# A two-layer decoder step on one core: GpSimd's and VectorE's orders in the FFN's first steps, the sums of squares at sub-layer ends, and the recurrence's projection quarters two by two

## The chip, the cores and the metric

The kernel runs on one core of a Trainium2 chip. The metric is the time of one execution on the device in microseconds. Each engine (TensorE or PE, VectorE or DVE, ScalarE or ACT, GpSimd or POOL, SyncE or SP) runs its own program in the order in which it is written; engines meet at semaphores only.

## The reference, cut

Two layers, 544 tokens (512 of a prompt and 8 x 4 of a sample group), D = 1024, FFN width 2816, all float32. Layer 0 mixes by causal pooling, layer 1 by a gated delta rule.

```python
for i in range(DEPTH):                                   # DEPTH = 2
    ng = p['norm_gains'][i]
    x = x + 0.5 * rmsnorm(swiglu(rmsnorm(x, ng[0]), gate[i, 0], up[i, 0], down[i, 0]), ng[1])
    h = rmsnorm(x, ng[2])
    y = pool_mixer(h, ...) if i % 2 == 0 else gated_deltanet(h, ...)
    x = x + rmsnorm(y, ng[3])
    x = x + 0.5 * rmsnorm(swiglu(rmsnorm(x, ng[4]), gate[i, 1], up[i, 1], down[i, 1]), ng[5])

def swiglu(h, w_gate, w_up, w_down):
    return (jax.nn.silu(h @ w_gate) * (h @ w_up)) @ w_down
```

The gated delta rule projects h to q, k, v, z (each head 128 wide), runs a short convolution, then for each chunk of tokens solves a triangular system and carries a state of 128 x 128 per head:

```python
v_new = ui - wi @ state
o = (qi * exp(gi)) @ state + ai @ v_new
state = state * exp(g_last) + k_dec.T @ v_new
```

## The kernel before

**Products.** Every float32 product w h is made of three reduced-precision matmuls: w_high h_high, w_low h_high, w_high h_low. A high part is a rounded copy that ScalarE writes (round_op L1635 for weights into w_h, high_quarter L1698 for activations into hhi); a low part is the difference of the value and its high part, one subtraction on GpSimd (low_of, L886) or VectorE (low_of, L2164; low_quarter, L2298, into hlo). Which of the two makes a weight's low part is said by by_vector. Tokens are worked in two halves of 272 (hf 0 and 1).

**Sub-layers.** There are six, r = 0 to 5: FFN (r = 0), pooling mixer (1), FFN (2), FFN (3), delta rule (4), FFN (5). The four FFNs are e = 0 to 3. An FFN is a list of steps. Step 0 is the first gate product (first_gate, L1074), steps 1 to 3 are plain products up, gate, up (plain, L1107), steps 4 to 7 the first chunk of the down projection (down, L1146). All later gate and up products go by a Strassen scheme with seven products in place of eight (seven, L1128). This needs three differences of quarters of the normed input, t1 to t3: VectorE makes tf (difference, L2292), ScalarE rounds it (high_difference, L1689), GpSimd makes its low part t_l (low_difference, L891). While the plain steps run, VectorE also applies the norm (normed, L2287), multiplies gate and up results (plain_gate L2269, plain_up L2273 and L2276, into hidf), makes the low part of the hidden values (hidden_low, L2282) and evicts down products (L2243 and L2245).

**Sub-layer ends.** For the RMSNorm after a sub-layer, ScalarE squares each of the 16 result tiles (L1654), VectorE adds most of the squares (add_square, L2206 and L2209, counted by ADDS), and TensorE sums over partitions by f32 matmuls with a matrix of 1/D: add_early (L1041) takes VectorE's sum, add_late (L1046) single squares. ScalarE makes the inverse root of it (post_root, L1599 and L1601), VectorE applies it and adds to x (post, L2228 and L2232). In the last down steps of every FFN the two halves are worked one after the other (down_halves, L1164), with the sums of half 0 among the products of half 1; `late_downs` lets VectorE evict the last four tiles between the pairs of post's operations. low_part (L2188) then makes the next sub-layer's hlo, low_first the low parts of the next FFN's step 0.

**The delta rule.** The projections are cut into quarters of 12 matmuls (quarter, L1344). A list `plan` gives for each quarter the steps of the recurrence that belong to its position, 48 positions for a group of four heads: level_z and level_ux (L1424, L1433, L1437) solve the triangular system by levels, right_side and keys_by_token (L1454, L1456) and new_values (L1463) carry the state, o_norm is L1483, low_products and att_products L1413, l2_sum L1397, and steps whose name begins with s_ belong to the sample group (s_update L1563). ScalarE, VectorE and GpSimd walk the same plan in an order of their own.

Of the kernel before, what the change touches and what calls it, by code (L numbers as in the profile page):

```python
# [129 lines left out]
def by_vector(step, i):  # L130
    return i in (A11, A22) if step.seven else step is steps_of(step.e)[0]


def low_counts():
    ops, ends, differences, pool, dve = [], [], [], 0, 0
    for step in STEPS:
# [8 lines left out]
        if at in (2, 3):  # L145
            for _ in range(4 - at):
                pool += 1
                differences.append(pool)
# [19 lines left out]
def build(nc, consts, I, O):  # L168
# [5 lines left out]
    with ctx:  # L174
# [337 lines left out]
        ADDS = [0, None, 10, 20, 30, 40]  # L512
# [356 lines left out]
        def _(pool):  # L869
# [23 lines left out]
            def ffn(e, r):  # L893
                steps = steps_of(e)
                for step in steps:
# [137 lines left out]
        def _(pe):  # L1033
# [5 lines left out]
            def add_early(r, hf):  # L1039
                pe.wait_ge(ss_add, ADDS[r] + ((9, 10) if r in (1, 4) else (8, 10))[hf])  # L1040
# [25 lines left out]
            def first_gate(step, r, late, freed):  # L1066
# [14 lines left out]
                for hf in range(2):  # L1081
# [71 lines left out]
            def down_halves(steps, r):  # L1153
                for hf in range(2):
                    for mt in range(4, KT):
# [3 lines left out]
                        for k in range(step.tiles):  # L1159
# [138 lines left out]
            def delta():  # L1298
# [64 lines left out]
                for at in range(len(plan)):  # L1363
                    quarter(at)
# [229 lines left out]
        def _(act):  # L1594
# [61 lines left out]
            def ffn(e, r):  # L1656
# [34 lines left out]
                def high_quarter(n):  # L1691
# [5 lines left out]
                    src = tf[:, 0] if n == 1 else y[:, ks, cols(hf)]  # L1697
# [462 lines left out]
        def _(dve):  # L2160
# [5 lines left out]
            def low_first(e, m):  # L2166
                for i in (2 * m, 2 * m + 1):
# [33 lines left out]
            def add_square(r, n):  # L2201
                mt, hf = TILES_F[n]
                before = ADDS[r] + (n - 3 if n < 9 else 7 if n == 9 else (8 if n == 12 else 9))
# [43 lines left out]
            def late_downs(e, r):  # L2247
                def between(k):
# [3 lines left out]
                    if k >= 4:  # L2252
                        add_square(r, n - 2)
                    if k == 4 and e == 1:
                        low_first(2, 0)
                return between

            def ffn(e, r):
# [26 lines left out]
                def normed(hf):  # L2285
                    for k in range(KT):
# [3 lines left out]
                def difference(n, a, b):  # L2290
                    dve.wait_ge(x_add, X_ADDS[r] + 18 + n)
                    dve.tensor_tensor(tf[:, n % 2 if n < 3 else 0], a, b, ALU.subtract).then_inc(x_add, 1)  # L2292

                def low_quarter(n):
                    ks, hf = ((slice(0, HK4), 0), (slice(0, HK4), 1), (slice(HK4, KT), 1), (slice(HK4, KT), 0))[n]
                    src = tf[:, 0] if n == 1 else y[:, ks, cols(hf)]
# [7 lines left out]
                for hf in range(2):  # L2304
# [7 lines left out]
                for n in range(1, 4):  # L2312
                    plain_up(steps[1], n // 2, n % 2)
                for n in range(4):
                    hidden_low(steps[1], n, n)
# [6 lines left out]
                for n in range(4):  # L2322
                    hidden_low(steps[3], n, n)
                dve.wait_ge(lo_pool, LOW_DIFFERENCES[3 * e + 2])
# [455 lines left out]
            for m in range(2):  # L2780
                low_first(0, m)
# [4 lines left out]
            for m in range(2):  # L2786
                low_first(1, m)
# [5 lines left out]
            post(2, 0, late_downs(1, 2))  # L2793
            low_part(3, 0)
            low_first(2, 1)
# [5 lines left out]
            low_first(3, 0)  # L2801
# [61 lines left out]
```

## Time and profile before

| what | value |
| --- | --- |
| median of 3 runs | 2488.42 us (2485.8 to 2612.95) |
| the profiled execution | 2487.07 us |
| its span in the trace | 2485.3 us |
| busy: PE, DVE, ACT, POOL | 94%, 65%, 43%, 45% of the span |
| TensorE's granted clock, mean | 0.975 of full speed |
| HBM | 207.20 MB read, 27.93 MB written |

The span is the trace's time from first to last instruction; 1.8 us of the execution lie outside it. The granted clock is the share of TensorE's full speed (2.4 GHz) that the chip allowed; its lower level is 1.2 GHz, 0.5 in such a column. A wait is the idle time of an engine, put down to the instruction that ended it.

### The profile page before, as it was taken

The numbers are of one execution on the slowest core, as the hardware profiler recorded it, in microseconds if no ns is written. First come the engines' busy times: TensorE is split into PE (matmuls) and PEld (weight loads), VectorE is DVE, ScalarE is ACT, GpSimd is POOL, SyncE is SP. The second block draws the span as 40 slices with busy tenths as digits, with TensorE's granted clock in tenths as the row PEclk, the third lists the DMA queues.
The fourth block names the chain that finished last, engine by engine and source line by source line (L and its number), as shares of the span: only waits on it lengthen the run. The fifth ranks groups of instructions, "written<-read, shape, count | busy, mean of one in ns | idle before, by whom it ended". The sixth has DMA issues, their size and how long they took to land. (4 is left out here: it accounts for less than half of the span.)

```text
span 2485.3 us, 45038 instructions
## 1 busy us (share of the span) xinstructions
PE 2332.6 (94%) x17619; PEld 2237.7 (90%) x17619; DVE 1627.3 (65%) x3004; ACT 1070.9 (43%) x2192; POOL 1107.6 (45%) x841
## 2 busy tenths in 40 slices
PE   7899999689999998999997899999999998899998
PEld 6899998589999988999986898888987987899997
DVE  5685584768585676765845666758567438686585
ACT  4353343334343453443446455363452224353343
POOL 2565562046565626655632022241223642665562
PEclk9999999899999999999999999999999999999999
DMA  3233323013333312332322434425445341233322
GB/s 121 63 104 98 102 82 104 20 43 100 114 104 109 96 59 79 106 97 86 99 75 63 112 84 120 126 59 133 127 118 146 101 158 61 73 94 98 103 81 75
DMA packets 294604, 235.57 MB, mean 95 GB/s; under 512 B 37339, under 2 KB 284788, under 8 KB 294107
## 3 DMA queue, kind: packets, MB, share of 16 engines
q1 hardware_dynamic: 294395, 232.71, 30.8%
q8 instruction: 141, 2.31, 0.4%
q14 instruction: 68, 0.56, 0.1%
HBM read 207.20 MB, written 27.93 MB: 95 GB/s over the span
## 5 line engine op out<-in xcount | busy, mean ns | idle before, releaser
L886 POOL TENSOR_TENSOR w_l<-raw,w_h 128x512 fp32r<-128x512 f32 (+1 forms) x416 | 522.1, 1275 | 330.9 <-ACT w_h L1635 330.9
L886 POOL TENSOR_TENSOR w_l<-wsum,w_h 128x512 fp32r<-128x512 f32 x216 | 332.6, 1548 | 364.3 <-ACT w_h L1635 364.3
L1146 PE MATMUL acc<-hid,w_h 128*128 128x272 f32 x2432 | 461.2, 288 | 8.4 <-DVE y L2243 8.4
L1635 ACT ACTIVATE w_h<-raw 128x512 fp32r<-128x512 f32 (+1 forms) x576 | 323.3, 585 | 166.2 <-PE acc L1146 113.7
L1146 PEld LDWEIGHTS acc<-hid,w_h 128*128 128x128 f32 x2432 | 382.8, 188 | 10.7 <-issue 10.7
L1146 PE MATMUL acc<-hid,w_l 128*128 128x272 f32 x1216 | 349.4, 287 | 0.0
L2245 DVE TENSOR_TENSOR y<-acc,y 128x272 f32<-128x272 f32 x192 | 84.7, 441 | 253.6 <-PE acc L1146 230.9
L1635 ACT ACTIVATE w_h<-wsum 128x512 fp32r<-128x512 f32 x216 | 134.9, 625 | 259.6 <-DVE wsum L2180 243.9
L1146 PEld LDWEIGHTS acc<-hid,w_l 128*128 128x128 f32 x1216 | 228.9, 188 | 0.0
L1344 PE MATMUL acc<-hhi,dhi 128*128 128x272 f32 (+1 forms) x1040 | 197.4, 311 | 13.0 <-POOL hlo L1022 3.7
L1685 ACT ACTIVATE hid<-hidf 128x272 fp32r<-128x272 f32 x176 | 75.2, 427 | 293.4 <-DVE hidf L2368 192.5
L2164 DVE TENSOR_TENSOR w_l<-raw,w_h 128x512 fp32r<-128x512 f32 x160 | 178.7, 1128 | 34.8 <-ACT w_h L1635 32.9
L1128 PE MATMUL acc<-hlo,w_h 128*128 128x272 f32 x624 | 180.2, 289 | 0.0
L1128 PE MATMUL acc<-hhi,w_l 128*128 128x272 f32 x624 | 179.7, 288 | 0.0
L1128 PE MATMUL acc<-hhi,w_h 128*128 128x272 f32 x624 | 179.5, 288 | 0.0
L1344 PE MATMUL acc<-hlo,dhi 128*128 128x272 f32 (+1 forms) x1040 | 178.1, 293 | 0.5 <-POOL hlo L924 0.4
L1344 PEld LDWEIGHTS acc<-hhi,dhi 128*128 128x128 f32 (+1 forms) x1040 | 149.3, 194 | 31.4 <-issue 14.4
L1344 PE MATMUL acc<-hhi,dlo 128*128 128x272 f32 (+1 forms) x1040 | 177.6, 294 | 0.0
L1128 PE MATMUL aux<-t_l,w_h 128*128 128x272 f32 x528 | 152.9, 290 | 0.0
L1128 PE MATMUL aux<-hlo,w_h 128*128 128x272 f32 x528 | 152.9, 290 | 0.0
L1128 PE MATMUL aux<-t_h,w_h 128*128 128x272 f32 x528 | 152.7, 289 | 0.0
L1344 PEld LDWEIGHTS acc<-hlo,dhi 128*128 128x128 f32 (+1 forms) x1040 | 150.5, 192 | 2.1 <-POOL hlo L924 1.5
(334 smaller groups left out, 6153.0 us busy)
## 6 DMA issues: line engine op xcount, KB each, us to landing
raw<-in_w_ffn_gate_dram SPq DMA_DIRECT2D x44, 1024.0 KB, 5.1
raw<-in_w_ffn_up_dram SPq DMA_DIRECT2D x44, 1024.0 KB, 5.1
raw<-in_w_ffn_down_dram SPq DMA_DIRECT2D x48, 768.0 KB, 4.4
wraw<-in_dn_w_in_dram SPq DMA_DIRECT2D x48, 512.0 KB, 4.0
raw<-in_w_ffn_down_dram SPq DMA_DIRECT2D x16, 512.0 KB, 3.3
room<-in_state_delta_dram SPq DMA_DIRECT2D x16, 512.0 KB, 4.8
out_delta_sample_dram<-room SPq DMA_DIRECT2D x16, 512.0 KB, 4.2
wraw<-in_dn_w_out_dram SPq DMA_DIRECT2D x16, 512.0 KB, 5.1
```

The costliest lines, as they stand in the source:

```text
L886: pool.tensor_tensor(w_l[o % RING][:, 0:n, :], source(step, i), w_h[o % RING][:, 0:n, :].bitcast(F), ALU.subtract)\
L1128: last = pe.matmul(banks[b], w[o % RING][:, k, :], h[:, k, :], start=(k == 0 and n == 0), stop=(k == HK4 - 1 and n == 2))
L1146: last = pe.matmul(acc[m][:, hf, 0:HT], w[o % RING][:, k % HK4, :], hid[:, k, z, cols(hf)], start=(k == 0 and j == 0), stop=(k == step.til ...
L1344: mm = pe.matmul(into[0:width, hf, 0:HT], w[s][:, kw, 0:width], a[:, ka, cols(hf)], start=(k == first and i == 0), stop=(k == last and i = ...
L1635: act.activation(w_h[o % RING][:, 0:n, :], source(step, i), ACT.Copy).then_inc(op_hi, 1)
L1685: act.activation(hid[:, tile, 0, cols(hf)], hidf[:, s, :], ACT.Copy).then_inc(hid_hi, 1)
L2164: dve.tensor_tensor(w_l[o % RING][:, 0:n, :], source(step, i), w_h[o % RING][:, 0:n, :].bitcast(F), ALU.subtract).then_inc(lo_dve, 1)
L2245: dve.tensor_tensor(yt, src, yt, ALU.add).then_inc(comb, 1)
```

## The change

- by_vector: of step 0's four weight low parts VectorE makes two and GpSimd two (before, VectorE all four). low_first has two operations, and its place moves: it no longer stands inside post.
- low_difference on GpSimd: t_l of differences 0 and 1 behind step 3's low parts (before, step 2's), of difference 2 behind step 4's (before, step 3's).
- The squares: VectorE adds those of tiles 2 to 9 only; TensorE takes tiles 12 to 15 by add_late, and add_early of half 1 and add_late 11 move into down_halves, each one place earlier.
- first_gate: the second tile's w_h product stands ahead of the first tile's w_l product.
- VectorE in the plain steps: plain_up of step 1 in the middle of the norm of half 1, each hidden_low right behind its hidden; difference 2 moves from ahead of step 3's ups to behind its last hidden_low. ScalarE: high_difference 2 and high_quarter 0 move behind step 3's hidden values and ahead of step 5's weights.
- TensorE in the delta rule: at even positions two quarters, at odd ones none; the steps keep their positions.

```diff
 def by_vector(step, i):
-    return i in (A11, A22) if step.seven else step is steps_of(step.e)[0]
+    return i in (A11, A22) if step.seven else step is steps_of(step.e)[0] and i < 2
...
-        ADDS = [0, None, 10, 20, 30, 40]
+        ADDS = [0, None, 8, 16, 24, 34]
...
-                    if step is steps[2]:
+                    if step is steps[3]:
                         low_difference(r, 0)
                         low_difference(r, 1)
-                    if step is steps[3]:
+                    if step is steps[4]:
                         low_difference(r, 2)
...
-                    pe.wait_ge(*low_ready(a + 1))
-                    products(0, hf, w_l, hhi)
                     pe.wait_ge(op_hi, b + 2)
                     freed(1, hf)
                     products(1, hf, w_h, hhi)
+                    pe.wait_ge(*low_ready(a + 1))
+                    products(0, hf, w_l, hhi)
                     products(0, hf, w_h, hlo, h_lo)
...
                             if hf and mt == 4 and k == HK4 - 1:
                                 add_late(r, 10)
+                                add_late(r, 11)
                             if hf and mt == 5 and k == 1:
-                                add_late(r, 11)
+                                add_early(r, 1)
...
             def sums_end(r):
-                add_early(r, 1)
-                add_late(r, 14)
-                add_late(r, 15)
+                for n in range(12, 16):
+                    add_late(r, n)
...
                 for at in range(len(plan)):
-                    quarter(at)
+                    if at % 2 == 0:
+                        quarter(at)
+                        quarter(at + 1)
                     for step, g, c in plan[at]:
...
-                high_difference(2)
                 for n in range(4):
                     hidden(steps[3], n, 2 * n + 2)
+                high_difference(2)
+                high_quarter(0)
                 for i in range(2):
                     round_op(steps[5], i)
-                high_quarter(0)
...
-                    if k >= 4:
-                        add_square(r, n - 2)
-                    if k == 4 and e == 1:
-                        low_first(2, 0)
...
-                    normed(hf)
+                    normed(hf, range(0, HK4))
+                    if hf:
+                        plain_up(steps[1], 0, 0)
+                    normed(hf, range(HK4, KT))
+                plain_up(steps[1], 0, 1)
                 difference(0, b12, b11)
-                plain_up(steps[1], 0, 0)
+                hidden_low(steps[1], 0, 0)
+                plain_up(steps[1], 1, 0)
                 difference(1, b22, tf[:, 0])
...
+                for n in range(4):
+                    plain_up(steps[3], n // 2, n % 2)
+                    if n:
+                        hidden_low(steps[3], n - 1, n - 1)
+                hidden_low(steps[3], 3, 3)
                 dve.wait_ge(lo_pool, LOW_DIFFERENCES[3 * e])
                 difference(2, b22, b12)
-                for n in range(4):
-                    plain_up(steps[3], n // 2, n % 2)
-                for n in range(4):
-                    hidden_low(steps[3], n, n)
-                dve.wait_ge(lo_pool, LOW_DIFFERENCES[3 * e + 2])
+                dve.wait_ge(lo_pool, LOW_DIFFERENCES[3 * e + 1])
                 difference(3, b21, tf[:, 1])
...
-            low_first(3, 0)
-            post(4, 0, lambda k: low_first(3, 1) if k == 4 else None)
+            low_first(3)
+            post(4, 0)
```

GpSimd's program at the first FFN, before: low parts of weights (w_l) and of the differences (t_l).

```order
L886 TENSOR_TENSOR w_l<-raw,w_h 128x512 x8
L891 TENSOR_TENSOR t_l<-tf,t_h 128x1088 x2
L886 TENSOR_TENSOR w_l<-raw,w_h 128x512 x4
L891 TENSOR_TENSOR t_l<-tf,t_h 128x1088
L886 TENSOR_TENSOR w_l<-raw,w_h 128x512 x8
```

The same rows in the changed kernel:

```order
L886 TENSOR_TENSOR w_l<-raw,w_h 128x512 x14
L891 TENSOR_TENSOR t_l<-tf,t_h 128x1088 x2
L886 TENSOR_TENSOR w_l<-raw,w_h 128x512 x2
L891 TENSOR_TENSOR t_l<-tf,t_h 128x1088
L886 TENSOR_TENSOR w_l<-raw,w_h 128x512 x6
```

The two t_l in a row stand six low parts later (two of these are step 0's, the others step 3's), and the third stands two low parts behind them, in place of four.

VectorE's program at the end of the first FFN's plain steps, before: the last product of step 3, its low parts, difference 3, low_quarter (hlo) and the evictions of step 4 (COPY).

```order
L2273 TENSOR_TENSOR hidf<-acc,stat 128x272
L2276 TENSOR_TENSOR hidf<-hidf,g 128x272
L2282 TENSOR_TENSOR hid<-hidf,hid 128x272 x4
L2292 TENSOR_TENSOR tf<-y,tf 128x1088
L2298 TENSOR_TENSOR hlo<-y,hhi 128x4x272
L2243 COPY y<-acc 128x272 x2
L2298 TENSOR_TENSOR hlo<-tf,hhi 128x4x272
```

The same place in the changed kernel, whose lines have other numbers (L2280 is hidden_low, L2290 difference, L2296 low_quarter, L2245 the copy):

```order
L2271 TENSOR_TENSOR hidf<-acc,stat 128x272
L2274 TENSOR_TENSOR hidf<-hidf,g 128x272
L2280 TENSOR_TENSOR hid<-hidf,hid 128x272 x2
L2290 TENSOR_TENSOR tf<-y 128x1088
L2290 TENSOR_TENSOR tf<-y,tf 128x1088
L2296 TENSOR_TENSOR hlo<-y,hhi 128x4x272
L2245 COPY y<-acc 128x272 x2
L2296 TENSOR_TENSOR hlo<-tf,hhi 128x4x272
```

Difference 2 now stands here, directly ahead of difference 3; two of the four hidden_low have left the stretch for an earlier place.

TensorE's program in a group of the recurrence, before, from level_ux of one position to the quarter two positions later (acc0 from dhi and dlo is a quarter, L1391 the tails, L1463 new_values, L1405 decay_sum).

```order
L1433 MATMUL aux1<-room 128x128 x4
L1437 MATMUL aux0<-room 128x128 x4
L1391 MATMUL acc1<-cst,y 27x128 x2
L1344 MATMUL acc0<-hhi,dhi1 128x272 x4
L1344 MATMUL acc0<-hhi,dlo1 128x272 x4
L1344 MATMUL acc0<-hlo,dhi1 128x272 x4
L1463 MATMUL aux1<-room 128x128 x4
L1405 MATMUL acc1<-cst,gates 128x128 x4
L1344 MATMUL acc0<-hhi,dhi0 128x272 x4
L1344 MATMUL acc0<-hhi,dlo0 128x272 x4
L1344 MATMUL acc0<-hlo,dhi0 128x272 x4
```

The same steps in the changed kernel, where level_ux is L1435 and L1439, the tails L1393, new_values L1465, decay_sum L1407:

```order
L1435 MATMUL aux1<-room 128x128 x4
L1439 MATMUL aux0<-room 128x128 x4
L1393 MATMUL acc1<-cst,y 27x128 x2
L1465 MATMUL aux1<-room 128x128 x4
L1407 MATMUL acc1<-cst,gates 128x128 x4
L1344 MATMUL acc0<-hhi,dhi0 128x272 x4
L1344 MATMUL acc0<-hhi,dlo0 128x272 x4
L1344 MATMUL acc0<-hlo,dhi0 128x272 x4
L1344 MATMUL acc0<-hhi,dhi0 128x272 x4
L1344 MATMUL acc0<-hhi,dlo0 128x272 x4
L1344 MATMUL acc0<-hlo,dhi0 128x272 x4
```

The quarter between level_ux and new_values is gone; it stands with its neighbour, ahead of this stretch, and the next two quarters follow one another behind decay_sum.

## Rows read from the trace of the kernel before

**Rows 1.** The page, part 1: busy us, share of the span, instructions.

```profile
PE 2332.6 (94%) x17619; PEld 2237.7 (90%) x17619; DVE 1627.3 (65%) x3004; ACT 1070.9 (43%) x2192; POOL 1107.6 (45%) x841
```

**Rows 2.** TensorE's waits over the span: total us, times, longest us.

```profile
PE acc L1107 <- POOL w_l L886: 16.9, 4, 4.3
PE acc L1074 <- ACT hhi L1613: 16.8, 13, 4.1
PE aux L1041 <- DVE stat L2209: 9.9, 3, 3.3
PE aux L1563 <- DVE room L2713: 8.5, 3, 3.5
PE acc L1146 <- DVE y L2243: 8.4, 8, 1.7
PE acc L1397 <- ACT stat L1976: 5.9, 4, 2.5
PE acc L1107 <- DVE hidf L2273: 5.6, 4, 1.5
PE acc L1074 <- DVE w_l L2164: 3.1, 1, 3.1
```

**Rows 3.** Windows, FFN 2's steps 2, 3: us, busy by engine, PEclk, DMA, GB/s.

```profile
921.00:937.50 16.50, 12.29 (x96) 12.07 (x96) 8.40 (x17) 9.36 (x17) 8.56 (x5) 0.93 0.03 10
937.60:951.95 14.35, 14.35 (x98) 14.35 (x99) 2.77 (x7) 1.29 (x3) 7.50 (x5) 0.84 0.23 74
```

**Rows 4.** Timeline of GpSimd there: start us, us, line, operation, count, idle before.

```profile
928.94 5.01 POOL L891 TENSOR_TENSOR t_l<-tf,t_h 128x1088 fp32r<-128x1088 f32 x2 [10.47 <-ACT t_h L1689]
933.90 6.02 POOL L886 TENSOR_TENSOR w_l<-raw,w_h 128x512 fp32r<-128x512 f32 x4
939.89 2.50 POOL L891 TENSOR_TENSOR t_l<-tf,t_h 128x1088 fp32r<-128x1088 f32 x1
```

**Rows 5.** Timeline of VectorE, same stretch and columns.

```profile
933.69 1.41 DVE L2292 TENSOR_TENSOR tf<-y 128x1088 f32<-128x1088 f32 x1
...
952.83 1.49 DVE L2282 TENSOR_TENSOR hid<-hidf,hid 128x272 fp32r<-128x272 f32 x4
954.24 2.39 DVE L2292 TENSOR_TENSOR tf<-y,tf 128x1088 f32<-128x1088 f32 x1
956.56 2.39 DVE L2298 TENSOR_TENSOR hlo<-y,hhi 128x1088 fp32r<-128x1088 f32 x1
```

**Rows 6.** Timeline of ScalarE, same stretch.

```profile
954.33 1.10 ACT L1698 ACTIVATE hhi<-y 128x1088 fp32r<-128x1088 f32 x1
```

**Rows 7.** Timeline of TensorE at the end of sub-layer 3.

```profile
1271.96 0.62 PE L1046 MATMUL aux<-stat,cst 128*128 128x272 f32 x2
...
1281.87 0.73 PE L1041 MATMUL aux<-stat,cst 128*128 128x272 f32 x2 [3.30 <-DVE stat L2209]
```

**Rows 8.** Timeline of VectorE at the ends of sub-layers 2 and 3.

```profile
882.79 1.28 DVE L2164 TENSOR_TENSOR w_l<-raw,w_h 128x512 fp32r<-128x512 f32 x2
...
1273.58 0.92 DVE L2228 SCALAR_TENSOR_TENSOR aux<-y,gpost,aux 128x272 f32<-128x272 f32 x2 [4.89 <-ACT aux L1601]
...
1275.45 0.90 DVE L2228 SCALAR_TENSOR_TENSOR aux<-y,gpost,aux 128x272 f32<-128x272 f32 x2
...
1279.17 0.43 DVE L2209 TENSOR_TENSOR stat<-stat 128x272 f32<-128x272 f32 x1
```

**Rows 9.** Timeline of TensorE in the recurrence, group 1.

```profile
1446.52 0.75 PE L1344 MATMUL acc<-hhi,dhi 128*128 128x272 f32 x4
...
1448.11 1.05 PE L1463 MATMUL aux<-room 128*128 128x128 f32 x8
...
1521.15 1.16 PE L1413 MATMUL acc<-x 128*128 128x128 f32 x8 [0.27 <-DVE room L2614]
```

**Rows 10.** Timeline of VectorE in the recurrence, group 1.

```profile
1447.19 0.68 DVE L2650 TENSOR_TENSOR room<-room,aux 128x512 f32<-128x512 f32 x1
...
1520.42 0.69 DVE L2614 TENSOR_TENSOR room<-acc,room 128x512 f32<-128x512 f32 x1
```

More of the change, by code:

```diff
@@ L144, in low_counts @@
         ends.append((pool, dve))
-        if at in (2, 3):
-            for _ in range(4 - at):
+        if at in (3, 4):
+            for _ in range(5 - at):
                 pool += 1
@@ L1039, in add_early @@
             def add_early(r, hf):
-                pe.wait_ge(ss_add, ADDS[r] + ((9, 10) if r in (1, 4) else (8, 10))[hf])
+                pe.wait_ge(ss_add, ADDS[r] + ((9, 10) if r in (1, 4) else (8, 6))[hf])
                 pe.matmul(aux[hf][:, 0:HT], ones_mean, ssacc[:, hf, :], start=True, stop=False)
@@ L1696, in high_quarter @@
                         act.wait_ge(x_add, X_ADDS[r] + 22)
-                    src = tf[:, 0] if n == 1 else y[:, ks, cols(hf)]
+                    src = tf[:, 1] if n == 1 else y[:, ks, cols(hf)]
                     act.activation(hhi[:, ks, cols(hf)], src, ACT.Copy).then_inc(h_hi, 1)
@@ L2164, in low_of, with low_first @@
                 dve.tensor_tensor(w_l[o % RING][:, 0:n, :], source(step, i), w_h[o % RING][:, 0:n, :].bitcast(F), ALU.subtract).then_inc(lo_dve, 1)
-            def low_first(e, m):
-                for i in (2 * m, 2 * m + 1):
+            def low_first(e):
+                for i in range(2):
                     low_of(steps_of(e)[0], i)
@@ L2202, in add_square @@
                 mt, hf = TILES_F[n]
-                before = ADDS[r] + (n - 3 if n < 9 else 7 if n == 9 else (8 if n == 12 else 9))
+                before = ADDS[r] + (n - 3 if n < 9 else 7)
                 dve.wait_ge(y_sq, 16 * r + n + 1)
@@ L2283, in hidden_low, with normed @@
                        .then_inc(hid_lo, 1)
-                def normed(hf):
-                    for k in range(KT):
+                def normed(hf, ks):
+                    for k in ks:
                         dve.scalar_tensor_tensor(y[:, k, cols(hf)], x[:, k, cols(hf)], gain(r // 3, 2 * (r % 3), k), rpre[:, hf, :],
@@ L2307, in ffn @@
                         plain_gate(steps[0], m, hf)
-                    normed(hf)
+                    normed(hf, range(0, HK4))
[3 more added lines that the diff above has]
+                plain_up(steps[1], 0, 1)
                 difference(0, b12, b11)
-                plain_up(steps[1], 0, 0)
+                hidden_low(steps[1], 0, 0)
+                plain_up(steps[1], 1, 0)
                 difference(1, b22, tf[:, 0])
-                for n in range(1, 4):
-                    plain_up(steps[1], n // 2, n % 2)
-                for n in range(4):
-                    hidden_low(steps[1], n, n)
+                hidden_low(steps[1], 1, 1)
+                plain_up(steps[1], 1, 1)
+                hidden_low(steps[1], 2, 2)
+                hidden_low(steps[1], 3, 3)
                 for n in range(4):
                     plain_gate(steps[2], n // 2, n % 2)
+                for n in range(4):
[3 more added lines that the diff above has]
+                hidden_low(steps[3], 3, 3)
                 dve.wait_ge(lo_pool, LOW_DIFFERENCES[3 * e])
                 difference(2, b22, b12)
-                for n in range(4):
-                    plain_up(steps[3], n // 2, n % 2)
-                for n in range(4):
-                    hidden_low(steps[3], n, n)
-                dve.wait_ge(lo_pool, LOW_DIFFERENCES[3 * e + 2])
+                dve.wait_ge(lo_pool, LOW_DIFFERENCES[3 * e + 1])
                 difference(3, b21, tf[:, 1])
@@ L2779, in _ @@
             low_part(0, 0)
-            for m in range(2):
-                low_first(0, m)
+            low_first(0)
             low_part(0, 1)
@@ L2785, in _ @@
             pool_mixer()
-            for m in range(2):
-                low_first(1, m)
+            low_first(1)
             for hf in range(2):
@@ L2793, in _ @@
             post(2, 0, late_downs(1, 2))
+            low_first(2)
             low_part(3, 0)
-            low_first(2, 1)
             post(2, 1)
```

4 lines of the change are left out of this document (2 added, 2 removed).

## The prediction

> **What bounds the kernel now.** I read the page's engine table first. TensorE is busy 94% of the span and VectorE 65% [rows 1], so time can only come from TensorE's gaps, and everything that makes TensorE wait anew costs its full length. The list of TensorE's waits [rows 2] names the gaps by line. Those that the change touches are: L1107 on GpSimd's low parts, 16.9 us in 4 waits, one in each FFN; L1107 on VectorE's hidf, 5.6 us in 4; L1146 on VectorE's y, 8.4 us in 8, two in each FFN; L1041 on the sum of squares, 9.9 us in 3; and part of L1074's 16.8 us on hhi. In the recurrence the list has short waits behind ScalarE (ACT) and VectorE (DVE) (L1397, L1563), each a few microseconds in all. That is the point to keep: the recurrence's steps are covered nearly everywhere today, and the cover is what the last part of the change rearranges.
>
> A wait can cost more than its length. In the windows of FFN 2, step 2 has 96 matmuls in 12.29 us busy, and step 3, which begins after the 4.2 us wait on GpSimd, has 98 records in 14.35 us at a mean granted clock of 0.84 [rows 3]: the clock stood at its lower level of 1.2 GHz for a part of it. The price of the drop is 14.35 - 12.29 = 2.06 us, so that wait costs about 6.3 us in each FFN.
>
> **The plain part.** Why the wait is there: GpSimd takes two t_l differences (5.01 us for 2) at 928.94, and only then step 3's low parts [rows 4]. The change puts these two differences one step later and lets GpSimd do its low parts first, and VectorE's operations on hidf come earlier. Removed in each FFN: 5.6 / 4 = 1.4 us on hidf, 16.9 / 4 = 4.23 us on w_l, 2.06 us of clock; 7.7 us.
>
> What is late next is step 5. Let T be the end of step 3. Then VectorE still has the last hidden and its low part (one of the four in the 1.49 us), ending at about T + 1.3 to 1.9; difference(2) now starts there (1.41 us alone [rows 5]), T + 3.2; ACT rounds it (1.1 us, as the activation of the same size in [rows 6]), T + 4.35; GpSimd's L891 takes 2.5 us [rows 4], T + 6.9. Only then come step 5's two low parts, at most 6.02 / 4 = 1.5 us each [rows 4]; I take 2.5 for both, T + 9.4. TensorE has step 4 to do, half a plain step, 12.29 / 2 = 6.1 us. So TensorE waits about 3.4 us before step 5, where it waited 8.4 / 4 = 2.1 us for y in two pieces, of which the longest is 1.7; the second one, 0.4, I take at 0.9. Given back: 3.4 - 1.7 + 0.9 - 0.4 = 2.2 us. A wait of 3.4 us is near the 4.2 us one in length, so I charge it the same 2.06 us of clock. Net 7.7 - 2.2 - 2.0 = 3.5 us in each FFN, **14 us** in four. Bounds: 22 us if the clock holds, nothing if VectorE's operations at that point stay as slow as today. They are slow: difference(3) takes 2.39 us where difference(2) takes 1.41 at the same size [rows 5], while GpSimd works.
>
> That row is where the Trainium skill bears: "SBUF — State Buffer", section "Who interferes with whom", says that a VectorE instruction with two SBUF inputs contends with a GpSimd instruction that reads SBUF. The trace agrees, with 2.39 against 1.41 us. By that rule the two low_quarter operations and GpSimd's L891 would again stand one behind the other in the new order, and the gain would be at the lower end of my bounds.
>
> **The boundaries.** At the end of an FFN VectorE runs a chain: post-norm, evictions of the last tiles, adds of squares, 1.86 us for each pair of tiles; TensorE's first use of the sum waits 3.30 us for it [rows 7]. Three edits shorten it. add_late 11 moves from 1271.96 [rows 7] up beside add_late 10, past 12 matmuls of the down projection, 12 x 12.29 / 96 = 1.5 us; ACT's root waits for it and VectorE's chain starts at 1273.58 behind that root [rows 8], so the chain starts up to 1.5 us earlier. Two add_squares of 0.35 us each (0.43 with their overlap [rows 8]) leave VectorE, one of them ahead of the last eviction. TensorE does two more f32 matmuls instead, 0.62 us each as the one at 1271.96 [rows 7] with its overlap, inside the gap. So 3.30 us shrinks by about 2.5: that is three places (the sub-layers 0, 3 and 5), 7.5 us. At sub-layer 2 the first two low parts, 1.28 us at 882.79 [rows 8], also leave the chain for after it: 3 us, less possible blocking of the hlo operations by GpSimd's two added low parts, so 3 with bounds 1.5 and 4. Before the last FFN two low parts leave the chain as well (1.2 us of the 16.8 in L1074's waits [rows 2]). At the start TensorE waits 3.1 us for VectorE's w_l [rows 2]; with two of the four on GpSimd and the second w_h product ahead I take 1.1. Sum 7.5 + 3 + 1.2 + 1.1 = 12.8, say **13 us**; bounds 7 and 18.
>
> **The recurrence.** Today each position is one quarter of a projection (12 matmuls) and then the steps of the recurrence for that position. At even positions the change sets two quarters, then the steps of both positions back to back. Merging saves nothing by itself: the matmuls are the same and run without gaps either way. What it changes is the distance between dependent steps. From an odd to the next even position the cover doubles; from an even to the odd one it goes: a quarter is 1.59 us (1446.52 to 1448.11 [rows 9]).
>
> Two pairs can be read. level_ux(2) to new_values(0): L1463 starts behind the quarter at 1448.11; without the quarter it could start at 1446.52, but VectorE's L2650, which makes its operand, starts at 1447.19 and takes 0.68 [rows 10], so it starts at about 1447.9: lost 1.3. att_products(0) to att_products(1): the second L1413 waits 0.27 us already with a quarter between [rows 9]; the bank is freed by L2614 at 1520.42 + 0.69 [rows 10]; lost about 1.6 to 1.7. Of the other even-to-odd pairs with a dependence I price right_side(1) to o_norm(0) and level_ux(7) to o_norm(2) at 0.65 each and s_products at 0.3, between 0 and the 1.59 of a quarter, near the 0.68 of a one-tile operation [rows 10] as each has one such operation between. Two more, level_ux(6) to new_values(2) and s_inverse to s_level_z, would lose 1.2 and 1.5, but a wait of 1.1 to 3.5 us on ACT or VectorE stands right behind (L1397, L1563 [rows 2]) and swallows it. So 1.3 + 0.65 + 0.65 + 0.3 + 1.7 = 4.6 us in each of three steady groups, 13.8. The first group, which waits for ACT anyway, loses nothing. In the last one the pairs of the sample's state (s_state to s_right_side, s_new_values to s_outputs) stand at odd distance one too, and no such wait covers them: about 8. Sum **21.5 us** lost; bounds 0 (all of it under waits that exist) and 40 (each charged a whole quarter, and the clock drops too).
>
> **Sum.** The profiled execution took 2487.07 us, 1.35 below the median of three. 2487.07 - 14 - 13 + 21.5 = 2481.6; I say **2481**. A measurement of this kernel can tell about 2% from no change, 49.8 us: below 2438.7 or above 2538.2.
>
> **Rivals.**
> - *The recurrence loses nothing.* The new short waits only eat the time that TensorE now waits behind ACT and VectorE, whose orders are unchanged. For it: waits of 5.9 and 8.5 us exist there [rows 2]. Against: TensorE is nearly gapless between them, and VectorE's answer comes 0.68 us and more after it starts. 2487.07 - 27 = 2460.
> - *Slower: the recurrence's new waits cost more than both other parts gain.* The place is the even-to-odd pairs; the point is 27 us. If each lost pair cost a whole quarter, and some of these gaps also brought the lower clock as the one of 4.2 us does [rows 3], it would lose 40 us: 2487.07 - 27 + 40 = 2500. The Trainium skill has a rule that speaks for this: "TensorE: Matmul & The Clock Gate", section "A second HAM failure mode: psum-queue depth-cycling", describes frequent small idles between matmul groups that let the clock swing between its two levels. The trace speaks against it so far: the recurrence has gaps of 0.3 us [rows 9] to 3.5 us [rows 2] already, and the drop that I priced stands behind one of 4.2 us.
> - *The plain part moves its wait and gains nothing.* The L891 of difference(2) and step 5's low parts take GpSimd 5 to 5.5 us after T + 4.35; with VectorE's blocked operations between, step 5 waits 7 us with the lower clock. Then 2487.07 - 13 + 21.5 = 2495.5, slower too.
> - *The change doesn't do what it says.* The orders show the quarters in pairs and GpSimd's differences moved, so this has no weight.
>
> **Chances.** The forecast's case, 2470 to 2490: 0.42. The recurrence loses nothing: 0.20. The recurrence loses 40: 0.16. The plain part gains nothing: 0.14. Something else, either side: 0.08. For 8 in 10 the range goes from 2457 (the first rival with 3 us more from the boundaries) to 2504 (the second with 4 us more lost); the likeliest case's own range is 2470 to 2490. All named cases lie within 2%; faster and slower by over 2% get 0.04 each from the rest.
>
> **What would show it.** Right: L1107 no longer waits for w_l or hidf; a wait of some 3.4 us stands before step 5 (L1146 in the new kernel too), on w_l rather than y; L1041's 3.3 us waits are gone, with L1046 waiting briefly for ACT's square; new waits of 1 to 2 us before new_values, att_products and o_norm, some 5 us in each steady group; clock 1.0 in step 3's window. Wrong: no new waits in the recurrence (first rival), a clock well below 0.98 there (second), or a wait at step 5 of 6 us and more (third).

## The result, and the profile after

The changed kernel takes 2497.31 us (median of 20 runs) against 2488.56 us before (20 runs). The ratio is 1.0034, 95% interval 1.0023 to 1.0044: slower by 0.3%, some 8 us, where I had forecast 6 us faster. The profiled execution took 2491.7 us, 4.6 above the one before. The changed kernel's single runs lie wider apart (2491.45 to 2506.98, one disturbed run left out) than those before (2485.43 to 2496.57, two left out), so a difference of 4 us between two medians says little below; the ratios carry the verdicts. The profiled run is one of the three shortest, so the trace shows about half of the 8 us.

That small number hides two large ones. The windows of the six stages of the changed kernel, cut at the first matmul of each (first FFN, pooling mixer, second and third FFN, delta rule, last FFN; the columns are start and end, length, then busy time of PE, PEld, DVE, ACT and POOL, the granted clock, DMA share and GB/s):

```profile
19.40:415.60 396.20, 387.88 (x3031) 383.91 (x3030) 269.79 (x482) 174.20 (x358) 217.12 (x161) 1.00 0.30 93
415.60:472.00 56.40, 37.32 (x136) 27.50 (x134) 40.52 (x74) 16.59 (x37) 5.72 (x5) 0.86 0.07 22
472.00:863.00 391.00, 385.17 (x2982) 381.23 (x2983) 274.57 (x495) 174.85 (x359) 217.31 (x161) 0.98 0.29 92
863.00:1259.80 396.80, 392.38 (x3048) 387.22 (x3046) 277.84 (x496) 176.71 (x360) 226.07 (x169) 0.99 0.28 86
1259.80:2082.00 822.20, 738.39 (x5377) 674.19 (x5376) 468.47 (x918) 340.89 (x710) 224.00 (x184) 0.95 0.37 106
2082.00:2489.20 407.20, 393.43 (x3030) 387.63 (x3030) 283.51 (x515) 177.36 (x363) 220.07 (x163) 0.98 0.27 86
```

The same six windows of the kernel before:

```profile
20.40:429.60 409.20, 392.75 (x3026) 387.81 (x3026) 271.95 (x486) 174.63 (x357) 218.69 (x161) 0.98 0.28 90
429.60:484.30 54.70, 36.84 (x136) 26.98 (x134) 39.74 (x76) 16.01 (x36) 1.95 (x3) 0.87 0.05 14
484.30:881.70 397.40, 387.11 (x2981) 382.55 (x2982) 272.58 (x489) 173.67 (x356) 218.76 (x161) 0.98 0.29 92
881.70:1289.30 407.60, 392.65 (x3041) 386.73 (x3039) 279.62 (x507) 178.05 (x363) 225.05 (x167) 0.99 0.27 84
1289.30:2069.60 780.30, 722.51 (x5378) 660.80 (x5376) 472.09 (x918) 344.39 (x710) 223.71 (x184) 0.97 0.39 111
2069.60:2485.30 415.70, 393.06 (x3026) 386.92 (x3026) 285.04 (x519) 177.60 (x363) 219.26 (x161) 0.98 0.27 85
```

The four FFNs with their ends gain 13.0, 6.4, 10.8 and 8.5 us, the start 1 and the mixer loses 1.7: 38 us gained. The delta rule goes from 780.3 to 822.2 us, 42 lost. Its two parts can be read from the same rows: the time in which TensorE is not busy goes from 780.30 - 722.51 = 57.8 to 822.20 - 738.39 = 83.8 us, 26 more; the same number of matmuls is busy for 15.9 us longer, and the mean clock falls from 0.97 to 0.95.

TensorE's waits in the changed kernel, to be held against [rows 2] (line numbers two or more higher: L1465 is new_values, L1485 o_norm, L1415 low_products and att_products, L1514 s_level_z, L1565 s_update, L1399 l2_sum):

```profile
PE acc L1146 <- POOL w_l L886: 13.7, 5, 3.3
PE acc L1074 <- ACT hhi L1615: 13.0, 12, 4.1
...
PE aux L1514 <- ACT spare L2055: 10.5, 4, 2.9
PE aux L1465 <- DVE room L2654: 9.8, 8, 1.5
...
PE acc L1415 <- DVE room L2618: 8.3, 4, 3.0
...
PE aux L1565 <- DVE room L2717: 6.3, 3, 2.6
PE acc L1344 <- DVE dlo L2520: 5.6, 5, 2.3
...
PE aux L1485 <- ACT room L2013: 4.5, 8, 0.6
```

L1107's waits on GpSimd and on hidf are gone, and so is L1041's on the squares. Step 5's wait for w_l (L1146) has come, 3.3 us in each FFN. New in the recurrence are the waits of L1465 and L1485. The quarters (L1344) waited for dlo, the low part of their weights, before as well, 2.8 us in 2 times; three times of 1.0 us have come to it. The waits of L1514 and L1415 are longer (4.5 and 4.0 us before), and L1565's is shorter (8.5 before).

### The profile page after: what moved, and what is told of

It is laid out like the page before. It is cut to its first block and busy times, and to the rows that moved or that the text cites. A ratio compares the mean times of both kernels' runs of the same rounds, so it can differ in the third digit from the quotient of the medians.

```text
span 2489.2 us, 45054 instructions
## 1 busy us (share of the span) xinstructions
PE 2342.0 (94%) x17635; PEld 2247.2 (90%) x17635; DVE 1621.0 (65%) x2988; ACT 1067.1 (43%) x2192; POOL 1113.0 (45%) x849
## 3 DMA queue, kind: packets, MB, share of 16 engines
q8 instruction: 141, 2.31, 0.4%
## 5 line engine op out<-in xcount | busy, mean ns | idle before, releaser
L1146 PE MATMUL acc<-hid,w_h 128*128 128x272 f32 x2432 | 465.9, 290 | 13.7 <-POOL w_l L886 13.7
L1146 PEld LDWEIGHTS acc<-hid,w_h 128*128 128x128 f32 x2432 | 387.6, 191 | 14.8 <-POOL w_l L886 14.8
L1146 PE MATMUL acc<-hid,w_l 128*128 128x272 f32 x1216 | 352.4, 290 | 0.0
L1146 PEld LDWEIGHTS acc<-hid,w_l 128*128 128x128 f32 x1216 | 232.0, 191 | 0.0
L1344 PE MATMUL acc<-hhi,dhi 128*128 128x272 f32 (+1 forms) x1040 | 198.5, 314 | 17.0 <-DVE dlo L2520 5.6
L2166 DVE TENSOR_TENSOR w_l<-raw,w_h 128x512 fp32r<-128x512 f32 x152 | 173.4, 1149 | 34.8 <-ACT w_h L1637 32.9
L1344 PEld LDWEIGHTS acc<-hhi,dhi 128*128 128x128 f32 (+1 forms) x1040 | 156.3, 201 | 35.6 <-issue 16.2
L1344 PE MATMUL acc<-hhi,dlo 128*128 128x272 f32 (+1 forms) x1040 | 182.2, 299 | 0.0
L1344 PE MATMUL acc<-hlo,dhi 128*128 128x272 f32 (+1 forms) x1040 | 181.5, 298 | 0.5 <-POOL hlo L924 0.4
L1344 PEld LDWEIGHTS acc<-hhi,dlo 128*128 128x128 f32 (+1 forms) x1040 | 155.9, 199 | 0.5
L1344 PEld LDWEIGHTS acc<-hlo,dhi 128*128 128x128 f32 (+1 forms) x1040 | 154.3, 197 | 1.9 <-POOL hlo L924 1.4
```

Of the source, the lines that this page charges most:

```text
L1146: last = pe.matmul(acc[m][:, hf, 0:HT], w[o % RING][:, k % HK4, :], hid[:, k, z, cols(hf)], start=(k == 0 and j == 0), stop=(k == step.til ...
L1344: mm = pe.matmul(into[0:width, hf, 0:HT], w[s][:, kw, 0:width], a[:, ka, cols(hf)], start=(k == first and i == 0), stop=(k == last and i = ...
L2166: dve.tensor_tensor(w_l[o % RING][:, 0:n, :], source(step, i), w_h[o % RING][:, 0:n, :].bitcast(F), ALU.subtract).then_inc(lo_dve, 1)
```

## The experiments

**e1 and e2: the pairs alone, and all but the pairs.** e1 is the changed kernel with

```diff
-                    if at % 2 == 0:
-                        quarter(at)
-                        quarter(at + 1)
+                    quarter(at)
```

> The changed kernel with the quarters one by one again (everything else of the change kept). Theory: the pairs alone make the recurrence longer, by waits of the dependent steps (about 26 us) and by TensorE's lower clock behind them (about 16 us); then the recurrence is 780 us again, L1465 on DVE and L1485 on ACT have no waits, and the time is 2487.1 - 38 = 2449 us. Rival: the recurrence is slower for another reason (what the FFN leaves behind, the chip's state): it stays near 822 us and the time near 2491.

Measured: 2455.38 us, ratio 0.9865 (0.9848 to 0.9882). The delta rule takes 783.7 us, 38 less than in the changed kernel and 3 more than before; new_values and o_norm (L1463 and L1483 here) are not in the list of waits.

e2 is the kernel before with those three lines the other way round.

> The kernel before with the pairs of quarters alone. Theory: +42 us in the recurrence and nothing elsewhere, 2487.1 + 42 = 2529 us. Rival (the pairs cost only the waits that I priced in the prediction): + 21.5, 2509 us. Rival (the two parts work on each other): the recurrence differs from the 822 us that it took in the changed kernel by over 5 us.

Measured: 2535.64 us, ratio 1.0195 (1.0174 to 1.0215), some 48 us; the profiled execution, the shortest of the four runs, 2529.27, 42 above the one before, and its delta rule takes 822.1 us against 822.2 in the changed kernel. The pairs make the whole loss, and the delta rule's loss doesn't depend on what the rest of the change does. My price for it, 21.5 us, is out.

Windows of the delta rule, cut at s_decay of each of the four groups, show where it lies. The first is the start, the next three are the steady groups, the last is the end. First before:

```profile
1289.30:1499.42 210.12, 186.11 (x1337) 171.92 (x1335) 122.62 (x233) 110.30 (x238) 38.87 (x35) 0.94 0.33 91
1499.42:1657.58 158.16, 149.60 (x1131) 136.16 (x1130) 106.69 (x196) 75.64 (x158) 40.71 (x36) 0.98 0.41 111
1657.58:1814.52 156.94, 148.30 (x1132) 135.68 (x1131) 105.73 (x196) 75.52 (x158) 40.90 (x36) 0.99 0.41 112
1814.52:1967.03 152.51, 143.75 (x1095) 131.96 (x1094) 94.29 (x189) 51.94 (x95) 55.37 (x44) 0.98 0.46 132
1967.03:2069.60 102.57, 94.75 (x688) 85.09 (x687) 42.75 (x104) 31.00 (x61) 47.87 (x36) 0.98 0.38 122
```

and with the whole change:

```profile
1259.80:1473.41 213.61, 186.54 (x1336) 172.44 (x1335) 122.95 (x233) 109.64 (x238) 38.85 (x34) 0.93 0.32 90
1473.41:1640.73 167.32, 153.26 (x1132) 139.35 (x1131) 106.65 (x196) 74.62 (x159) 40.67 (x36) 0.96 0.39 105
1640.73:1808.01 167.28, 153.22 (x1132) 139.33 (x1131) 106.70 (x196) 74.62 (x159) 40.68 (x36) 0.96 0.39 105
1808.01:1972.23 164.22, 147.12 (x1095) 134.91 (x1095) 89.61 (x189) 51.27 (x96) 55.91 (x45) 0.95 0.42 123
1972.23:2082.00 109.77, 98.24 (x688) 88.17 (x687) 42.57 (x104) 30.74 (x61) 47.89 (x36) 0.95 0.35 114
```

The start loses 3.5 us, the three groups 9.2, 10.3 and 11.7, the end 7.2. In the first steady group TensorE stands still for 8.6 us before and for 14.1 us after, 5.5 more; I had priced 4.6. But the same matmuls are busy 3.7 us longer as well, at a lower clock, and for that I had charged nothing. In the changed kernel TensorE's timeline has it within this group:

```profile
1421.23 1.13 PE L1465 MATMUL aux<-room 128*128 128x128 f32 x8 [1.25 <-DVE room L2654]
...
1506.05 0.41 PE L1514 MATMUL aux<-spare 32*32 32x32 f32 x8 [2.95 <-ACT spare L2055]
...
1507.80 1.11 PE L1344 MATMUL acc<-hhi,dlo 128*128 128x272 f32 x4
...
1510.47 0.67 PE L1344 MATMUL acc<-hhi,dlo 128*128 128x272 f32 x4
...
1537.36 1.02 PE L1344 MATMUL acc<-hhi,dhi 128*128 128x272 f32 x4 [1.02 <-DVE dlo L2520]
1538.18 1.11 PE L1344 MATMUL acc<-hhi,dlo 128*128 128x272 f32 x4
```

The wait before new_values (L1465) is 1.25 us, where I had 1.3. The one before L1514, which I had let L1563's wait swallow, is 2.95 us, 1.5 more than before, and behind it a row of four matmuls takes 1.11 us instead of 0.67 until 1510.5: the granted clock is 0.50 from 1507 to 1510, TensorE's lower level of 1.2 GHz. The quarter at 1537.36 shows a wait that I had not thought of at all: its weights are not split yet. VectorE's timeline, before (L2701 and L2516) and after (L2705 and L2520, the split into dlo):

```profile
1547.97 0.29 DVE L2701 TENSOR_TENSOR spare<-spare,aux 128x128 f32<-128x128 f32 x1
...
1555.19 1.21 DVE L2516 TENSOR_TENSOR dlo<-wraw,dhi 128x1024 fp32r<-128x1024 f32 x1
```
```profile
1528.87 0.29 DVE L2705 TENSOR_TENSOR spare<-spare,aux 128x128 f32<-128x128 f32 x1 [2.12 <-PE aux L1528]
...
1536.10 1.21 DVE L2520 TENSOR_TENSOR dlo<-wraw,dhi 128x1024 fp32r<-128x1024 f32 x1
```

The quarter is the first of its pair and stands behind the same matmuls as before. What has moved is the step of an even position, s_state (L1528): it now stands behind both quarters of its pair. VectorE waits 2.12 us for it where it did not wait before, and the split, which ends 8.4 us behind that answer in both kernels, ends at 1537.31. Between s_state and this quarter TensorE has four quarters now and had five. So this is lost cover too, by way of VectorE's order. The clock falls behind that wait as well.

**e3: pairs only where nothing depends.**

```diff
-                    if at % 2 == 0:
+                    if (at // 2 * 2 - 4) % 48 in (10, 14, 20, 24, 26, 28, 30, 36, 38):
+                        quarter(at)
+                    elif at % 2 == 0:
```

> The changed kernel with pairs only where the odd position's steps need nothing from the even one's (single quarters at positions 10, 14, 20, 24, 26, 28, 30, 36 and 38 of each group). Theory (a pair costs only by the cover it takes from a dependent step): like the kernel without pairs, 2449 us, within 4. Rival (a pair costs or saves by itself, by longer bursts, evictions or the clock): off from that kernel by over 6 us.

Measured: 2459.46 us, ratio 0.9880 (0.9865 to 0.9896) against 0.9865 for e1: at the edge of the interval, 4 us in the medians and 4.3 in the delta rule (788.0 against 783.7). The theory holds to that size: the nine pairs that take the cover of a dependent step carry 34 of the 38 us by which the delta rules of the changed kernel and of e1 differ (822.2 against 783.7). My list of them had a hole, though: the trace of e3 has a wait of 1.5 us at level_ux (L1437 there) on VectorE in each of the three steady groups, which neither e1 nor the changed kernel has. No gain shows from the pairs that are left.

**e7: single quarters at positions 28 and 30 only.** The same edit as e3 with the list (28, 30).

> The changed kernel with single quarters at positions 28 and 30 of each group only. Theory (the longer wait before L1514, 2.9 us, brings the lower clock behind it, the one of 1.4 us before did not): in each steady group the wait of att_products goes from 1.8 to 0.3 and that of L1514 from 2.9 to 1.4, and the 3.3 us at 1.2 GHz behind it go too, 4.7 us in each of three groups, 14 in all: 2497 - 14 = 2483 us. Rival (the clock falls for another reason, such as the longer bursts): the low stretch stays, and 9 us are gained, 2488.

Measured: 2487.79 us, ratio 0.9998 (0.9986 to 1.0009) against 1.0034, some 9 us less; in the trace the delta rule takes 815.0 us, 7.2 less. The group's window is

```profile
1476.06:1639.67 163.61, 151.87 (x1131) 137.82 (x1131) 107.77 (x196) 74.62 (x159) 39.52 (x36) 0.97 0.40 107
```

3.7 us shorter than in the changed kernel: 2.3 us less idle (11.74 against 14.06) and 1.4 us less busy. I had expected 4.7. L1514's wait (L1516 here) is back at 1.47 us, and the low clock behind it is gone, here and in the second steady group; the wait for att_products only went from 1.8 to 1.0. In the third steady group the clock still falls, 7 us behind the same wait (1.45 us there), after matmuls at full speed:

```profile
1833.03 0.41 PE L1516 MATMUL aux<-spare 32*32 32x32 f32 x8 [1.45 <-ACT spare L2057]
...
1841.02 1.11 PE L1344 MATMUL acc<-hlo,dhi 128*128 128x272 f32 x4
```

So the time is the one that the rival gave, 2488; its sign, a low stretch that stays, is there in one group of three. That the longer wait brings the low clock is shown for two groups, and the 14 us that I had built on it were too many.

**e8: pairs at odd positions.**

```diff
-                    if at % 2 == 0:
+                    if at == 0:
+                        quarter(at)
+                    elif at % 2:
```

> The changed kernel with pairs at odd positions: two quarters, then the steps of an odd and the next even position. Theory (a pair costs by the steps whose cover it takes): now even-to-odd neighbours have two quarters between them and odd-to-even ones none; new_values, o_norm and the first pair of att_products no longer wait, but s_level_z to s_level_u and the second pair of att_products do, about 3 to 4 us in each group: between, 2465 to 2475 us. Rival (pairs cost by the bursts or by earlier claims on weights and banks, whatever the parity): 2490 or more.

Measured: 2479.54 us, ratio 0.9964 (0.9949 to 0.9979), profiled 2471.98; the delta rule takes 801.8 us. Half of the loss goes with the parity. What stays is not what I had named: neither s_level_u nor the second att_products leads its list, but quarters, which wait 2.35 us for dlo in two groups, 3.4 and 3.7 us for ScalarE at the end of a group, and in all 3.5 us longer than before for hlo. Here the first quarter of a set of weights does stand one position earlier than before. These quarters' waits are 14 us longer than before, while TensorE's idle time is 11.6 us longer in all, since others shrank, and its matmuls are busy 9.8 us longer. So most of the waiting that stays is theirs and not lost cover of steps; but new_values and o_norm, which I had freed of waits, still wait 2.9 and 2.2 us in all (9.8 and 4.5 in the changed kernel).

**e4 and e5: the plain part alone, the boundaries alone.** e4 has the change's edits to low_difference, difference, plain_up, hidden_low and ScalarE's order; e5 those to by_vector, ADDS, add_early, add_late, first_gate and low_first.

> The kernel before with the change's plain part alone (GpSimd's differences one step later, VectorE's and ScalarE's orders). By the prediction's price, 3.5 us in each FFN, 14 in all: 2473 us. By the stages of the changed trace, where the FFNs and their ends gained 38 us together and the ends were priced at 13: 25 us, 2462. Step 5 waits 3.3 us for w_l in either case; they differ in whether the lower clock follows.

Measured: 2470.91 us, ratio 0.9931 (0.9911 to 0.9950), 17 us: nearer to the prediction's price than to the stages'.

> The kernel before with the change's boundary edits alone (step 0's low parts, the squares, first_gate, low_first). By the prediction's price 13 us: 2474. By difference (the kernel without pairs against the plain part alone) 11 to 16 us, so 2471 to 2476. Rival (the two parts overlap: what one gains the other would have gained too): less than 8.

Measured: 2473.01 us, ratio 0.9941 (0.9922 to 0.9959), 15 us. The two add up to the 33 us of e1. One part of e5 goes the wrong way: the mixer's stage takes 56.4 us here and 54.4 in e4. VectorE's and GpSimd's timelines in e5 say why:

```profile
446.50 2.58 DVE L2739 TENSOR_TENSOR winv<-hp 128x1356 f32<-128x1356 f32 x1
```
```profile
446.39 3.81 POOL L886 TENSOR_TENSOR w_l<-raw,w_h 128x512 fp32r<-128x512 f32 x2
```

The two low parts that by_vector gave to GpSimd fall into the mixer, and the operation beside them takes 2.58 us, where later ones of the same line take 1.55 to 1.57.

**e6: the third difference still later.** e1 with

```diff
-        if at in (3, 4):
-            for _ in range(5 - at):
+        if at in (3, 5):
+            for _ in range(2 if at == 3 else 1):
...
-                    if step is steps[4]:
+                    if step is steps[5]:
                         low_difference(r, 2)
```

> The changed kernel with single quarters, and GpSimd's third difference behind step 5's low parts in place of step 4's. Theory (step 5 waits 3.3 us only because L891 stands ahead of its low parts on GpSimd): that wait goes in all four FFNs, 13 us, and with it the lower clock behind three of them, some 5 us: 2455.4 - 18 = 2437 us. Rival (VectorE's low_quarter, or the evictions behind it, are late as well): TensorE waits for y or hlo in its place, and at most 5 us are gained, 2450.

Measured: 2450.19 us, ratio 0.9842 (0.9821 to 0.9863), which overlaps e1's. The rival's time was right, its cause was not: TensorE still waits for w_l in the first place (9.0 us in 8 times, 2.1 us for y). Step 5's wait falls from 3.3 to 1.83 us, as ScalarE rounds step 5's weights only behind its two other operations, and up to 1 us comes back at the tiles behind.

**e9 and e10: weights rounded earlier, the mixer's low parts back, the difference last.** e9 is e6 with

```diff
-    return i in (A11, A22) if step.seven else step is steps_of(step.e)[0] and i < 2
+    return i in (A11, A22) if step.seven else step is steps_of(step.e)[0] and (i < 2 or step.e == 1)
...
-                for n in range(4):
+                for n in range(3):
                     hidden(steps[3], n, 2 * n + 2)
-                high_difference(2)
-                high_quarter(0)
                 for i in range(2):
                     round_op(steps[5], i)
+                hidden(steps[3], 3, 8)
+                high_difference(2)
+                high_quarter(0)
...
-                for i in range(2):
+                for i in range(4 if e == 1 else 2):
                     low_of(steps_of(e)[0], i)
```

> The kernel of e6 (single quarters, third difference behind step 5's low parts) with two more edits: ScalarE rounds step 5's weights ahead of the last hidden of step 3, so that GpSimd makes their low parts while step 4 runs; and at the FFN behind the pooling mixer VectorE makes all four of step 0's low parts again, so that GpSimd works on none of them beside the mixer's VectorE operations. Theory: step 5 no longer waits for w_l (1.8 us in each FFN) but for y, 1.3 to 1.7 us, as it did before the change; the pooling mixer's stage goes from 56.4 us back to 54.7, as L2739 takes 1.56 us again and not 2.58: 2450.2 - 1.7 - 1 to 4 = 2444 to 2448 us. Rival for the mixer (its longer stage comes from the earlier start, not from GpSimd's port): it stays at 56.4 and TensorE waits 3.3 us at L1279 as before.

Measured: 2452.17 us, ratio 0.9862 (0.9841 to 0.9882): no better than e1. The mixer's half of it worked: 54.4 us, and L2746 (L2739 above) takes 1.56 us. The other half turned against itself. GpSimd's, VectorE's and TensorE's timelines in the first FFN of e9:

```profile
84.31 2.54 POOL L891 TENSOR_TENSOR t_l<-tf,t_h 128x1088 fp32r<-128x1088 f32 x1 [3.67 <-ACT t_h L1689]
```
```profile
85.27 2.73 DVE L2295 TENSOR_TENSOR hlo<-y,hhi 128x1088 fp32r<-128x1088 f32 x1 [0.79 <-ACT hhi L1698]
88.04 0.79 DVE L2244 COPY y<-acc 128x272 f32<-128x272 f32 x2
```
```profile
88.63 0.36 PE L1146 MATMUL acc<-hid,w_h 128*128 128x272 f32 x1 [3.40 <-DVE y L2244]
```

With the low parts out of the way GpSimd starts L891 early enough to meet low_quarter (L2295), as it did in the changed kernel and did not in e6, where low_quarter takes 1.29 us. That ends behind L891, at 88.0, and the evictions that TensorE waits for stand behind it. e10 is e9 with the third difference behind step 7 (`(3, 7)` and `steps[7]`).

> The kernel of e9 with GpSimd's third difference behind step 7's low parts (before: step 5's). Theory (in e9 L891 started 4 us behind step 3 and held VectorE's low_quarter, 2.73 us for 1.29, so that y came 3.4 us late): low_quarter takes 1.3 us, the evictions end before step 4 does, and the wait before step 5 goes in all four FFNs, 13 us, with the lower clock behind it, 5: 2452.2 - 18 = 2434 us. Rival (another GpSimd operation, the low parts of steps 6 and 7, holds VectorE at the same place): y is late by 2 us and more, 2445 to 2452.

Measured: 2446.79 us, ratio 0.9839 (0.9824 to 0.9854), the lowest median here, 1.6% below the kernel before, though its interval and e6's overlap nearly whole. low_quarter takes 1.29 us again, but the wait for y is still 1.97 us. GpSimd's and VectorE's timelines in e10:

```profile
80.31 2.53 POOL L886 TENSOR_TENSOR w_l<-raw,w_h 128x512 fp32r<-128x512 f32 x2 [3.97 <-ACT w_h L1635]
```
```profile
81.82 1.32 DVE L2273 TENSOR_TENSOR hidf<-hidf,g 128x272 f32<-128x272 f32 x1
```

L2273 took 0.44 us at 78.80 and takes 1.32 beside step 5's low parts; differences, roundings and low_quarter follow on it one behind the other. So by this row 0.9 us of the 1.97 come from GpSimd, and the rest from the length of that chain. The time lies in the rival's range, 2445 to 2452, and another GpSimd operation did hold VectorE, though not the one that the rival named.

## Why the prediction was wrong

**The plain part** held. Step 3's window of FFN 2 now has the full clock, against 0.84 in [rows 3]:

```profile
909.20:921.47 12.27, 12.27 (x100) 12.27 (x99) 5.79 (x9) 2.77 (x6) 7.95 (x5) 1.00 0.28 87
```

The new wait before step 5 measured 3.3 us for the 3.4 predicted, on w_l. The chain was the one that I had added up but for its last term, which came out by luck. GpSimd's, VectorE's and TensorE's timelines there:

```profile
926.03 2.55 POOL L891 TENSOR_TENSOR t_l<-tf,t_h 128x1088 fp32r<-128x1088 f32 x1 [8.88 <-ACT t_h L1691]
928.54 2.31 POOL L886 TENSOR_TENSOR w_l<-raw,w_h 128x512 fp32r<-128x512 f32 x1
```
```profile
926.98 2.75 DVE L2296 TENSOR_TENSOR hlo<-y,hhi 128x1088 fp32r<-128x1088 f32 x1 [0.79 <-ACT hhi L1700]
```
```profile
930.91 0.59 PE L1146 MATMUL acc<-hid,w_h 128*128 128x272 f32 x1 [3.28 <-POOL w_l L886]
```

I had taken 2.5 us for both of step 5's low parts; TensorE starts behind the first alone, and that takes 2.31. low_quarter and L891 did stand one behind the other, as I had feared, 2.75 us against 1.29 without (e6), but the evictions behind low_quarter, from 929.76 on, were done before w_l was, so it cost TensorE nothing here. A reading of mine was off as well: difference(2) did not run alone in [rows 5]; GpSimd's low parts began at 933.90 beside it [rows 4]. Where GpSimd stands idle, in the changed kernel, it takes 1.28 us, so the sum hardly changes. The gain was 17 us (e4; 12 to 22 by its interval) for 14: behind the first FFN's 3.3 us wait the clock stayed at full speed, and behind those of the others it fell as charged.

**The boundaries** held as well: 15 us (e5; 10 to 19) for 13. GpSimd's two added low parts did block VectorE in low_part behind sub-layer 2, as I had feared; in the changed kernel's timeline of VectorE it takes 5.45 us, where it took 3.38 before:

```profile
864.89 5.45 DVE L2190 SCALAR_TENSOR_TENSOR hlo<-x,gains,hhi 128x272 fp32r<-128x272 f32 x8
```

but TensorE has other products there and doesn't wait for it. It was in the mixer, which I had not looked at, that they cost 1.7 to 2 us. The Trainium skill's rule that I cited for the plain part, "SBUF — State Buffer", section "Who interferes with whom", is what happens there too: by that rule an operation with two inputs in SBUF meets GpSimd's reads, and the trace agrees, with 2.58 us in e5 against 1.56 in e9, where VectorE makes these low parts; no other of their edits lies in the mixer.

**The recurrence** failed, in its size: 42 us lost for 21.5, in the trace; the step that failed is the sum of its lost cover. Of the 42 us, 26 are waits and 16 are slower matmuls, so most of what was missing is the lower clock, a term that I had put at nothing in the forecast, though I had charged it in the FFN: 3.7, 4.9 and 3.4 us in the three steady groups and 3.5 in the end. e7 shows that one of the first group's two new stretches goes when the wait before it goes back from 2.9 to 1.5 us. The waits were short by less: 5.5, 5.4 and 8.3 us in the steady groups for 4.6 each. I had let the wait of s_inverse to s_level_z be swallowed by L1563's, but that fell by 0.8 us only (3.46 to 2.62), and the 1.5 us stayed; the other one, at new_values(2), was swallowed (l2_sum's wait of 1.1 us on stat is gone). The wait for the split weights, 1.0 us in each group, was not on my list. The start, where I had put nothing, lost 3.5 us. The end lost 7.2 for about 8, which is luck in part: half of it is clock. The prices of the single pairs were right where I could read them: 1.25 for 1.3 at new_values, 1.5 for 1.6 to 1.7 at att_products, 0.56 for 0.65 at o_norm.

So the slower rival, 40 us lost in the recurrence, was the case that came, with 16 us of it from the clock and 26 from waits. Its time was 2500 us: the median lies 3 us below, the profiled execution 8, as the FFNs gained 11 us more in the trace than its sum had and the recurrence lost 2 more. Of its two reasons the clock is the one that came; the pairs did not cost a whole quarter each (1.59 us), as the prices above show. I had given it 0.16 against 0.42 for half the loss. The Trainium skill's rule that I weighed there ("TensorE: Matmul & The Clock Gate", section "A second HAM failure mode: psum-queue depth-cycling") says that frequent small idles between groups of matmuls cost clock beyond their length; the trace agrees in that the recurrence's mean clock fell from 0.97 to 0.95 with more and longer idles. I had set it aside because the recurrence had gaps up to 3.5 us already and I placed the drop behind one of 4.2 us only. The trace of the kernel before speaks against that reason: its wait of 3.46 us at L1563 has a drop behind it, with a granted clock of 0.51 over 7 us:

```profile
1570.61 3.75 PE L1563 MATMUL aux<-room 32*128 32x512 f32 x4 [3.46 <-DVE room L2713]
```
```profile
1570.00:1577.00 7.00, 6.39 (x16) 3.88 (x17) 6.86 (x21) 0.32 (x1) 1.89 (x1) 0.51 0.57 118
```

## What to carry to other kernels

On an in-order engine that interleaves independent work with a chain of dependent steps, the independent work is the cover; moving it together saved nothing here and took the cover from the dependent steps between. It also delays what another engine does behind its answer to such a step, as the split of the weights here. Price such a regrouping pair by pair, look in the trace of before for the waits behind which the clock falls and charge new waits in that stage for it, and take no wait as swallowed by a later one unless the trace shows that both end at the same event. When two edits of opposite sign share a change, as here 33 us of gain and 42 of loss, time them apart before judging either: without the pairs this change is 1.35% faster than the kernel before.

## What the runs showed of the hardware beyond that

The lower clock does not follow from the length of the last wait alone. In the changed kernel it fell behind a wait of 1.02 us at 1537.36, whereas in e7 a wait of 1.47 us (L1516) passed without a drop in the first steady group, and in the third the drop came 7 us behind the same wait. What sets it stays open here; no run was made for it.
